# Gathering the small products of attention heads into one place per slab, on one Trainium2 core

## The reference

```
h = rmsnorm(x, norm_g)
(a_q, a_ckv, i_q, i_k, i_w, a_gate, b_q, b_k, b_v, b_gate, c_q, c_gate, mix_gate) = split(h @ w_in)
ckv = rmsnorm(a_ckv);  a_k, a_v = split(ckv @ w_kv_up)
oa = top-k attention, 6 heads of 128 (q, k normed per head; the index scores pick the keys)   * silu(a_gate)
ob = sliding window attention, 12 heads of 64 on 2 key heads, with a sink                      * silu(b_gate)
m_k, m_v = split(rmsnorm(mem) @ w_mem_kv)
oc = attention over 256 memory tokens, 4 heads of 128                                          * silu(c_gate)
merged = sigmoid(..) * (oa @ w_up_a) + sigmoid(..) * (ob @ w_up_b) + sigmoid(..) * (oc @ w_up_c)
x = x + merged @ w_o
```

## Time and profile before

| | before |
|---|---|
| median of 3 runs | 2068.66 us (2068.5 to 2068.67) |
| the profiled execution, its own time | 2068.58 us |
| its span in the trace | 2066.8 us |
| TensorE busy | 2052.3 us, 99% |
| DVE, ACT, POOL busy | 66%, 46%, 4% |
| DMA | 386.99 MB, mean 187 GB/s |

### The profile page before, as it was taken

The page is one execution under the profiler, slowest core; times in us unless marked ns, Lnnn a source line. Parts: engine busy times, 40 slices in busy tenths (PEclk is TensorE's granted clock), DMA queues, the critical chain, the costliest instruction groups (busy, mean ns, idle before and its releaser), DMA issues.

```text
span 2066.8 us, 29541 instructions
## 1 busy us (share of the span) xinstructions
PE 2052.3 (99%) x10650; PEld 1741.9 (84%) x10650; DVE 1364.8 (66%) x1823; ACT 950.7 (46%) x1223; POOL 82.3 (4%) x90
## 2 busy tenths in 40 slices
PE   9999999999999999999999999999999999999998
PEld 7888898877778888999888888888888888888886
DVE  6666766566767555578999766486556646645655
ACT  6545444555554444433444644453333333333343
POOL 0000102001002000002000000000000000000000
PEclk9999999999999999999999999999999999999999
DMA  8588555556557655555666565556666566556653
GB/s 299 183 191 196 177 157 178 183 159 192 166 172 241 190 183 183 176 175 159 189 195 197 182 235 183 184 167 192 196 188 193 188 193 188 187 194 188 192 191 105
DMA packets 267869, 386.99 MB, mean 187 GB/s; under 512 B 12411, under 2 KB 151513, under 8 KB 267228
## 3 DMA queue, kind: packets, MB, share of 16 engines
q1 hardware_dynamic: 264876, 374.83, 58.3%
q0 software_dynamic: 2576, 10.41, 2.0%
q10 hardware_dynamic: 304, 0.27, 0.0%
HBM read 382.79 MB, written 2.54 MB: 186 GB/s over the span
## 4 chain that ended last, share of the span: by engine, by line
PE 97%; SPq 1%; DVE 1%; ACT 0%; issue 0%; DMA 0%; DVEq 0%; ACTq 0%
PE acc L551 19%; PE acc L553 18%; PE acc L552 18%; PE acc L578 18%; PE acc L576 10%; PE acc L570 2%; PE acc L568 2%; PE acc L569 2%; PE acc L574 1%; PE aux L1394 1%; PE aux L1473 1%; SPq L447 0%; PE aux L1404 0%; PE acc L523 0%; PE acc L522 0%
## 5 line engine op out<-in xcount | busy, mean ns | idle before, releaser
L464 DVE TENSOR_TENSOR low_rows<-stage_rows,high_rows 128x1024 fp32r<-128x1024 f32 x435 | 537.7, 1238 | 412.9 <-ACT high_rows L456 407.6
L456 ACT ACTIVATE high_rows<-stage_rows 128x1024 fp32r<-128x1024 f32 x435 | 459.5, 1058 | 579.6 <-PE acc L553 531.2
L464 DVE TENSOR_TENSOR w_low<-stage,w_high 128x1024 fp32r<-128x1024 f32 (+1 forms) x272 | 329.6, 1221 | 232.4 <-ACT w_high L456 228.8
L456 ACT ACTIVATE w_high<-stage 128x1024 fp32r<-128x1024 f32 (+1 forms) x272 | 284.5, 1048 | 425.6 <-PE acc L578 309.4
L578 PE MATMUL acc<-u,w_high 128*128 128x512 f32 x960 | 264.7, 394 | 0.0
L551 PE MATMUL acc<-high_rows,f_pair 128*128 128x512 f32 x496 | 193.0, 389 | 0.0
L552 PE MATMUL acc<-low_rows,f_pair 128*128 128x512 f32 x496 | 192.9, 389 | 0.0
L553 PE MATMUL acc<-high_rows,f_pair 128*128 128x512 f32 x496 | 192.9, 389 | 0.0
L578 PEld LDWEIGHTS acc<-u,w_high 128*128 128x128 f32 x960 | 163.1, 189 | 20.1
L578 PE MATMUL acc<-hT,w_high 128*128 128x512 f32 x645 | 177.6, 394 | 0.0
L576 PEld LDWEIGHTS acc<-u,w_low 128*128 128x128 f32 x1024 | 156.7, 188 | 22.0
(11 more groups left out here) (386 smaller groups left out, 3297.7 us busy)
## 6 DMA issues: line engine op xcount, KB each, us to landing
stage_rows<-in_w_in SPq DMA_DIRECT2D x160, 512.0 KB, 3.7
stage<-in_w_in SPq DMA_DIRECT2D x136, 512.0 KB, 3.6
stage<-in_w_up SPq DMA_DIRECT2D x128, 512.0 KB, 4.0
stage_rows<-in_w_down SPq DMA_DIRECT2D x128, 512.0 KB, 4.3
stage_rows<-in_w_o SPq DMA_DIRECT2D x64, 512.0 KB, 3.9
stage_rows<-in_w_mem_kv SPq DMA_DIRECT2D x16, 512.0 KB, 9.4
stage_rows<-in_w_pool_out SPq DMA_DIRECT2D x16, 512.0 KB, 4.2
stage_rows<-in_w_conv_out SPq DMA_DIRECT2D x16, 512.0 KB, 4.6
```

Source lines behind the costliest of these rows:

```text
L456: act.activation(high[:, pr, 0:kt, 0:p.cols], src[:, slot, 0:kt, 0:p.cols], ACT.Copy).then_inc(high_done, 1)
L464: dve.tensor_tensor(low[:, pr, 0:kt, 0:p.cols], src[:, slot, 0:kt, 0:p.cols], high[:, pr, 0:kt, 0:p.cols].bitcast(F32), ALU.subtract).then ...
```

## The change

All of a head's three groups of products now stand beside the same slab, with those of its neighbours: the turn comes four slabs after the logits and the product with the values eight slabs after, and as heads start every four slabs, beside one slab stand the values of head h - 2, the turn of head h - 1 and the logits of head h, in that order. ACT's copy moves with the turn, DVE's copy out with the values; the exponentials and `scale_probs` stay at n + 1 and n + 2. The sums get a table of their own, which puts them where heads or other small products stand. The key turns of `early` stand together beside slab 8, and the work on the index key moves by one slab. DVE scales both tiles of x beside slab 7. The identity turns are 11 and 6 in place of 6 and 8.

```
-        SQUARE_AT = {"early": {1: 0, 6: 1, 9: 2, 13: 3, 17: 4}, "late": {17: 5, 21: 6, 25: 7, 45: 8, 49: 9}}
+        SQUARE_AT = {"early": {2: 0, 7: 1, 9: 2, 13: 3, 17: 4}, "late": {20: 5, 24: 6, 28: 7, 44: 8, 48: 9}}
+        SUM_AT = {"early": {3: (0,), 8: (1,), 14: (2, 3), 21: (4,)}, "late": {21: (5,), 25: (6,), 29: (7,), 45: (8,), 49: (9,)}}
...  ACT head_steps
-                h = stages(HEAD_AT[name], n, 5)
+                h = stages(HEAD_AT[name], n, 4)
...  TensorE, the start
-                keep_running(8 if q else 6, 2)
+                keep_running(6 if q else 11, 2)
...  TensorE sums
-                i = stages(SQUARE_AT[name], n, 1)
-                if i is None:
-                    return
+                for i in SUM_AT[name].get(n, ()):
+                    head_sums(i)
...  TensorE beside_early
-                if n == 0:
+                if n == 1:
...
-                if n == 5:
+                if n == 6:
...
-                if n in (6, 7):
-                    p = n - 6
+                if n == 8:
                     pe.wait_ge(s("ck_scaled"), 1)
                     pe.wait_ge(s("iw_ready"), 1)
-                    turn_keys(mk_rows, 2 + p, p, "ck_turned")
+                    for p in range(2):
+                        turn_keys(mk_rows, 2 + p, p, "ck_turned")
...  TensorE head_steps
-                for lag, stage in ((7, weigh_values), (5, turn_probs), (0, head_logits)):
+                for lag, stage in ((8, weigh_values), (4, turn_probs), (0, head_logits)):
...  DVE beside_mem
-                if n in (7, 8):
-                    if n == 7:
-                        chain_inverse(0)
-                    dve.tensor_scalar(x_in[:, n - 7, :], x_in[:, n - 7, :], rs_col("x", n - 7), None, ALU.mult).then_inc(s("x_scaled"), 1)
+                    chain_inverse(0)
+                    for t in range(2):
+                        dve.tensor_scalar(x_in[:, t, :], x_in[:, t, :], rs_col("x", t), None, ALU.mult).then_inc(s("x_scaled"), 1)
...  DVE head_steps
-                for lag, stage in ((7, copy_out), (2, scale_probs), (0, head_logits)):
+                for lag, stage in ((8, copy_out), (2, scale_probs), (0, head_logits)):
...  DVE beside_early: centring 0 to 1, variance 2 to 3, inverse 3 to 4, scaling the keys 4 to 5
-                if n == 6:
+                if n == 7:
                     dve.wait_ge(s("ik_spread"), 1)
...  DVE and ACT, the chain of aq and ckv: 19 and 20 to 22 and 23
```

More of the change, by code:

```diff
@@ L923, in beside_early @@
                             head_squares("ck", mk_rows, P, t, h, C_HEADS)
-                if n == 3:
+                if n == 4:
                     chain_root(2)
-                if n == 8:
+                if n == 9:
                     act.wait_ge(s("ck_turned"), 2)
@@ L932, in beside_early @@
                         act.activation(ckv_pair[:, a, 0, :], early[:, E_CKV + a, :], ACT.Copy, scale=column("kv_norm_g", a)).then_inc(s("ckv_high"), 1)
-                if n == 20:
+                if n == 23:
                     chain_root(3)
@@ L1302, in sum_steps, with head_sums @@
             def sum_steps(name, n):
-                i = stages(SQUARE_AT[name], n, 1)
-                if i is None:
-                    return
+                for i in SUM_AT[name].get(n, ()):
+                    head_sums(i)
+            def head_sums(i):
                 kind, r = SQUARED[i]
@@ L1806, in beside_early @@
                     dve.wait_ge(s("iw_ready"), 1)
-                if n == 2:
+                if n == 3:
                     dve.wait_ge(s("summed"), 1)
@@ L1814, in beside_early @@
                         dve.tensor_scalar(k_diag[:, t, :], ident[:], rs_col("ik", t), None, ALU.mult).then_inc(s("ik_diag"), 1)
-                if n == 4:
+                if n == 5:
                     for t in range(2):
@@ L1833, in beside_early @@
                     dve.sem_inc(s("ckv_ready"), 1)
-                if n == 19:
+                if n == 22:
                     dve.wait_ge(s("summed"), 5)
                     chain_var(3, ("aq", 0, sums("aq", 2 * A_HEADS), 1.0, P * EPS), ("ckv", 0, sums("ckv", 2), 1.0 / KV_RANK, EPS))
-                if n == 20:
+                if n == 23:
                     chain_inverse(3)
```

## The result

The changed kernel takes 2078.31 us (median of 5 runs, 2078.22 to 2080.75) against 2068.66: ratio 1.0048, interval 1.0034 to 1.0063, slower by 9.65 us. The prediction was 2071.0 with a range of 2067.0 to 2073.4. The profiled execution has a span of 2076.4 (before 2066.8) and a mean granted clock of 0.997 (before 0.999).

A forecast was written before the change was run, and what follows sets the result against it. TensorE, busy 99% of the span, was taken as the bound. The terms -0.6 - 0.9 - 0.3 + 0.4 - 0.2 - 2.1 + 6.1 = +2.4 on 2068.58 gave 2071.0 us, range 2067.0 to 2073.4.

The forecast's parts named there:

- What bounds the kernel: Whole span: TensorE, busy 99%, is the bound; whatever it doesn't have to wait for or pass counts one for one.
- The turns wait for the probabilities: Heads from `w_up_a` slab 28 and `w_up_c` slabs 7, 27: TensorE waits 2.4, 2.3 and 1.4 us, together +6.1.
- The start: First identity turns around `mem_in`: two turns less at half clock save 0.6 us, bounds -0.3 and -0.9.
- x: Turns of x near 43 to 45: scaling the second tile a slab earlier removes TensorE's wait, -0.9 us.
- Early: Index key work in `early`: the wait for `ikw` goes, -0.3; a longer wait for the scaled index key, +0.4.
- The waits of the values: Products with the values, now four slabs behind their turn: the wait for copied probabilities goes, -0.2 us.
- Fewer breaks: Groups of small products in TensorE's stream: 43 breaks fewer at 0.05 each, -2.1 us, bounds -0.4 and -3.4.
- The slower rival: Small-product groups: gathering saves nothing, 0.00 a break, giving +4.5 us, 2073.1, slower by the bound; chance 0.16.

The follow-up runs named there:

- the three turns later: Changed kernel with turn and ACT's copy of three heads five slabs behind their logits instead of four: 2068.76 us, ratio 0.9998 against the kernel before.

## Why the prediction was wrong

- **What bounds the kernel**: right. Each wait of TensorE came out at the end one for one, and more.
- **The turns wait for the probabilities** (+6.1): right in place, number and size: 2.55, 2.42 and 1.40 for 2.4, 2.3 and 1.4. The step that failed is the price of such a wait: the prediction has the stream stand behind the waiting turn and adds nothing but the wait's length. But a TensorE that stood still could go on at half clock. That is 1.6 behind the first wait, and another 1.5 at 1358 in the profiled execution. It was weighed for the start only, where it counted as a gain, and never put to the waits that the change adds.
- **The wait for `bkv`** (+2.2) was in no term. The change moved ACT's gate by 0.6 against DVE; the prediction followed semaphores, and this wait comes from none. It could have been seen in the trace of the kernel before: DVE's scalings 0.74, POOL's product 0.59 behind the first.
- **The start** (-0.6): failed. -0.65 was there at 9.8 and nothing at 31.6. The clock did rise sooner, but the bounds left out what TensorE waits for next: the second `mem_in` at 8.16, and the slab landing at 28.3. Alone, the edit gave nothing.
- **x** (-0.9): right where it stands; 0.4 of it is given back at 61 in the changed kernel, a limit that the prediction didn't look for.
- **Early** (-0.3 and +0.4): right, -0.32 and +0.43.
- **The waits of the values** (-0.2): right, the wait is gone.
- **Fewer breaks** (-2.1): the right sign and somewhat too large. 1.6 in the changed kernel, the 0.2 of the copied probabilities apart, against 2.1; with the three turns later, 1.8 for the 25 breaks behind `bkv` alone, where 0.05 each would be 1.3. A B head went from 2.49 to 2.39, as forecast. The rate came from B heads and doesn't hold everywhere: 14 of the 43 breaks were removed between 97 and 340, among the A heads and the sums, and gave 0.19, 0.01 each; the 28 behind 350 gave 1.4, 0.05 each. The slower rival (gathering saves nothing) is refuted.

The sum: +2.4 predicted; +0.6 for the start, +0.4 for x, +2.2 for `bkv`, +3.1 for the clock, +0.5 for the breaks and +0.4 for longer waits make +9.6, as measured. The second fall of the clock, at 1358, is not shown to be caused by the change: the kernel before has it in about half of its runs. That the first comes from the wait is shown, by the same wait filled.

## What to carry to other kernels

Where TensorE is the bound, price a new wait at its length and at a possible half clock behind it (here up to 3.1 us behind a wait of 2.6); where it can't be removed, turns of the identity in it kept the clock here, and made the runs agree too. When an edit shifts engines by a few tenths, look for the pairs that share something without a semaphore, DVE and GpSimd above all: a shift of 0.5 us was enough here to change whose instruction starts first. A gain ahead of a transfer that lands at a fixed time is none; follow it to the next landing before it enters a sum.

## What was not expected of the hardware

- The granted clock fell to half behind idle waits of 2.4 to 2.6 us in some executions and not in others (behind the first wait in three of three traces, behind the second in two of three, at a cost of 1.6 to 3.1; behind the wait of 2.4 for `bkv` in the one trace that has it). It did not fall behind the third wait, of 1.4, nor behind the waits of 2.0 for `bkv` in four traces. Behind the pair of waits of 1.4 and 1.1 at 1350 it fell in about half of the runs.
- Four DVE operations of 128x64 took 0.74 us with POOL's product starting 0.59 behind the first, and 2.79 with it 0.08 behind.
